# High and low fp32r parts for the recurrence gates' products in a one-core decoder step

## The chip, the cores and the metric

The kernel runs on one core of a Trainium2 chip. The metric is the device time of one execution in microseconds (us), from several timed executions. One further execution was taken by the hardware profiler, and the rows below come from it.

## The reference

One step of a hybrid decoder: 512 prompt tokens and 32 sample tokens (8 sequences of 4), model width 1024. A mixer with two branches is followed by a mixture of experts. The change lies in the second branch, the RG-LRU recurrence, whose two gates are block-diagonal products: eight blocks of 128 channels, each with one 128x128 matrix per gate.

```python
def block_diag_linear(x, w, b):
    xb = x.reshape(x.shape[:-1] + (H_B, BLK_B))          # H_B = 8 blocks of BLK_B = 128
    y = jnp.einsum('bshi,hij->bshj', xb, w) + b
    return y.reshape(x.shape)

def rg_lru(x, h0, lam, w_a, b_a, w_x, b_x):
    r = jax.nn.sigmoid(block_diag_linear(x, w_a, b_a))
    i = jax.nn.sigmoid(block_diag_linear(x, w_x, b_x))
    log_a = -LRU_C * r * jax.nn.softplus(-lam)
    a = jnp.exp(log_a)
    mult = jnp.sqrt(-jnp.expm1(2.0 * log_a))
    bt = mult * (i * x)
    ...                                                   # h[t] = a[t] * h[t-1] + bt[t]

def mixer_sublayer(...):
    u, v, xr, g_a, g_b = jnp.split(rms_norm(x, norm_g) @ w_in, SPLITS, axis=-1)
    y_a = gelu(u) * spatial_gating(layer_norm(gelu(v)))
    xc, new_buf = causal_depthwise_conv(xr, conv_buf, conv_w, conv_b)    # 4 taps
    y_b, h_last = rg_lru(xc, h0, ...)
    merged = jax.nn.sigmoid(g_a) * y_a + jax.nn.sigmoid(g_b) * y_b
    return x + merged @ w_out, h_last, new_buf, v_rows
```

## The kernel before

The program is written engine by engine, each engine with its own instruction list in a fixed order; semaphores tie the lists together, and no scheduler moves anything. Its stages in time are: normalising and transposing the tokens, the v projection (8 weight units), a loop over 8 channel tiles of 128 channels, the output projection (16 units), routing, and the experts, whose weights stream in by DMA.

The projections are made in fp32r, a format in which TensorE needs one pass for a product. To keep fp32 accuracy a product is split: ScalarE writes the high part of a weight unit (`split_hi`, line 697: `wh` from `raw`), VectorE the low part (`split_lo`, line 906: `wl` = `raw` - `wh`), and `product` (lines 1475 to 1477) makes high times high, high times low and low times high into the same PSUM bank.

The loop over channel tiles (`channel_tile` on TensorE, `channel` on VectorE, a loop of the same length on ScalarE) has four projection units per tile, p = 0 to 3, each 24 fp32r products of 128x512:

- First the 32 sample rows of all four units (line 1594), which need the four raw weight tiles that the sync engine's queue loads ahead (line 474).
- Unit 0 gives the recurrence's input. ScalarE copies it to `XR` (semaphore `xr_ev`), and VectorE makes the four-tap convolution `XC` from it (lines 1056 to 1070) and then raises `conv_done`.
- Unit 1 gives u, and unit 2 the first branch's output gate.
- After unit 2 TensorE waits for `conv_done` and makes the two recurrence gates (lines 1626 and 1627): for each gate w a plain fp32 product of `gw[:, w]` with the 512 prompt columns of `XC`, and one with the 32 sample columns. `gw`, two 128x128 matrices, is loaded for each tile by GpSimd's queue (line 624) once the tile before has used it. In the first tile the spatial mixing of the v branch (lines 1578, 1583) stands between unit 1 and unit 2.
- Unit 3 gives the second output gate.
- ScalarE turns the gates into a and the square root that the recurrence needs; for that it waits for `gates_mm` and, later, for the end of unit 3. VectorE then makes the scan and the merge (lines 1085 to 1112), splits weights in between, and goes round the loop.

On VectorE, `own.then(instruction)` issues an instruction and waits until it has finished. Tiles 0 to 6 are a hardware loop; the last one is written out after it, with the output projection's first `split_lo` calls in between.

Of the kernel before, what the change touches and what calls it, by code (L numbers as in the profile page):

```python
# [22 lines left out]
P = 128  # L23
D = 1024
KT = D // P
SEQ = 512
# [39 lines left out]
F32 = mybir.dt.float32  # L66
F32R = mybir.dt.float32r
# [3 lines left out]
ALU = mybir.AluOpType  # L71
# [37 lines left out]
def build(nc, x, wmix, wgate, chan, wst, bs, rows, wr, br, wmoe, y, vp, vs, st):  # L109
# [3 lines left out]
    def at(name, offset, shape, dt=F32):  # L113
        return nc.alloc_sbuf_tensor_at(name, shape, dt, offset=BASE + offset)

    K = 1024
# [58 lines left out]
    top = [181 * K]  # L175

    def small(name, shape, dt=F32):
        size = 4
        for n in shape[1:]:
            size *= n  # L180
        t = at(name, top[0], shape, dt)
        top[0] += -(-size // 32) * 32
        return t
# [6 lines left out]
    late = top[0]  # L190
# [3 lines left out]
    gw = small("gw", [P, 2, P])  # L194
# [30 lines left out]
    rstd = small("rstd", [P, TILES])  # L225
    ssa = small("ssa", [P, TILES])
    lg = small("lg", [P, TILES, NL])
    r4 = small("r4", [P, TILES, NG])
    oh = small("oh", [P, TILES, NG])
    r1 = small("r1", [P, 8, TILES])  # L230
    key = small("key", [P, TILES, NE])
    ohe = small("ohe", [P, 2, TILES, NE])
    mcnt = small("mcnt", [P, TILES, NE], BF16)
    cum = small("cum", [P, TILES + 1, NE], BF16)
    onesb = small("onesb", [P, P], BF16)
# [29 lines left out]
    with ExitStack() as ctx:  # L265
        ps = ctx.enter_context(nc.psum_tensor("ps", [P, 8, 512], F32))

        def sem(name):
            return ctx.enter_context(nc.semaphore(name))
# [8 lines left out]
        gw_in = sem("gw_in")  # L278
# [619 lines left out]
        def _(d):  # L898
            own = Steps(d, dve_s)
# [150 lines left out]
            def channel(j, last):  # L1050
# [2 lines left out]
                n0 = UNITS_V  # L1053

                d.wait_ge(gates_mm, FIRST + j)
                own.then(d.tensor_copy(xrs[:, :, 0:3], col(C_ST, 24).rearrange("p (b s) -> p b s", b=DB)))
                d.wait_ge(xr_ev, FIRST + j * 2 + 2)
                own.then(d.tensor_scalar(XC[:, 0:SEQ], XR[:, 3:3 + SEQ], col(C_W0 + 3), col(C_CB), ALU.mult, ALU.add))
                own.then(d.tensor_scalar(smp(XC), xrs[:, :, 3:7], col(C_W0 + 3), col(C_CB), ALU.mult, ALU.add))
                for t in range(3):  # L1060
# [4 lines left out]
                    if t < 2:  # L1065
                        own.then(i)
                own.then(i)
                sj = so[:, bass.ds(j, 1), :].rearrange("p a c -> p (a c)")
                d.tensor_copy(sj[:, 9:12], XR[:, SEQ:SEQ + 3])
                d.tensor_copy(sj[:, 12:36].rearrange("p (b s) -> p b s", b=DB), xrs[:, :, 4:7]).then_inc(conv_done, 1)  # L1070
# [47 lines left out]
                    split_lo(0, 2, j * 4 + (n0 + 7))  # L1118

            with d.Fori(0, KT - 1) as j:  # L1120
                own.enter(j, 25)
                channel(j, False)
                own.leave(KT - 1)
            channel(KT - 1, True)

            def add_rows(half, p, bank):
# [338 lines left out]
        def _(pe):  # L1465
# [7 lines left out]
            def product(out, sh, sl, mh_, ml_, start, stop):  # L1473

                pe.matmul(out, sh, mh_, start=start, stop=False)  # L1475
                pe.matmul(out, sl, mh_, start=False, stop=False)  # L1476
                return pe.matmul(out, sh, ml_, start=False, stop=stop)  # L1477
# [36 lines left out]
            def nothing(*_):  # L1514
                pass
# [53 lines left out]
            def z_mixing():  # L1569

                pe.wait_ge(masks, 7)
                pe.wait_ge(v_gelu, 2 * TILES)
                pe.wait_ge(v_ready, 1 + TILES)
                for c8 in range(KT):
                    if c8 >= 4:
                        pe.wait_ge(z_ready, c8 - 3)
                    for c in range(NT):
                        i = pe.matmul(ps[:, ZB[c8 % 4], c * P:(c + 1) * P], v[:, c, c8 * P:(c8 + 1) * P], wsT[:, c8 // 2, :],  # L1578
                                      start=True, stop=True)
                    i.then_inc(z_mm, 1)  # L1580
                pe.wait_ge(z_ready, 5)
                for c8 in range(KT):
                    i = pe.matmul(ps[:, ZB[0], c8 * S:(c8 + 1) * S], v[0:S, NT, c8 * P:(c8 + 1) * P], bdiag[:, c8 // 2, :],
                                  start=True, stop=True)
                i.then_inc(z_mm, 1)
                pe.wait_ge(z_ready, KT)

            def channel_tile(j, z_here):
                for s in range(RAW):
                    pe.wait_ge(raw_in[s], j * 16 + 48)  # L1590
                pe.wait_ge(sproj_sb, FIRST + j)
                for k in range(KT):
                    q = k % 4
                    i = pe.matmul(ps[S * q:S * q + S, 6, :].rearrange("p (u c) -> p u c", u=4), xs[:, k, :], raw[:, :, k, :],  # L1594
                                  start=k < 4, stop=k >= 4, tile_position=(0, S * q), skip_group_check=True)
                i.then_inc(sproj, 1)
                for p, freed in enumerate((xr_ev, u_ev, ga_ev, None)):
                    pe.wait_ge(hi_ready, j * 4 + (UNITS_V + p + 1))
                    pe.wait_ge(lo_ready, j * 4 + (UNITS_V + p + 1))
                    if z_here and p < 2:  # L1600
                        pe.wait_ge(v_gelu, 2 * TILES - 2 + p)
                    if freed is not None:
                        pe.wait_ge(freed, FIRST + j * 2)
                    else:
                        pe.wait_ge(merged, FIRST + j)
                    for k in range(KT):
                        c = slice(k * P, k * P + P)
                        i = product(ps[:, p, :], wh[:, p % 2, c], wl[:, p % 2, c], xh[:, k, :], xl[:, k, :], k == 0, k == KT - 1)
                    i.then_inc(unit_done, 1)
                    if p == 1 and z_here:  # L1610
                        z_mixing()
                    if p == 0:

                        pe.wait_ge(sproj_sb, FIRST + j + 1)
                        pe.wait_ge(gates_ev, FIRST + j * 4)
                        for u in range(4):
                            i = pe.matmul(ps[:, 7, u * S:(u + 1) * S], sp[:, u * P:(u + 1) * P], fold[:], start=True, stop=True)
                        i.then_inc(sproj_T, 1)
                    if p == 2:
                        pe.wait_ge(conv_done, FIRST + j + 1)  # L1620
                        pe.wait_ge(gw_in, j * 16 + 16)
                        pe.wait_ge(sq_sb, j + 1)
                        pe.wait_ge(z_ready, 2 * KT)
                        pe.wait_ge(gates_ev, FIRST + j * 4)
                        for w in range(2):
                            pe.matmul(ps[:, 4 + w, :], gw[:, w, :], XC[:, 0:SEQ], start=True, stop=True)  # L1626
                            i = pe.matmul(ps[:, 7, (4 + w) * S:(5 + w) * S], gw[:, w, :], XC[:, SEQ:TA], start=True, stop=True)
                        i.then_inc(gates_mm, 1)

            channel_tile(0, True)  # L1630
            with pe.Fori(1, KT) as j:
                channel_tile(j, False)
# [140 lines left out]
            for s in range(2):  # L1773
                for p in range(TILES):
                    r = rowsof(TILE_AT[p])
                    for part in range(3):
                        l = pe.matmul(ps[:, 4, 0:PAIRS], posh[0:r, s, p, :], rsk[0:r, part, s, p, :],
                                      start=s + p + part == 0, stop=s == 1 and p == TILES - 1 and part == 2)
# [180 lines left out]
```

## Time and profile before

| what | value |
|---|---|
| median of 3 runs | 658.03 us (654.76, 658.03, 659.07) |
| the profiled execution's own time | 657.93 us |
| span of the profiled execution | 656.3 us |
| TensorE busy | 602.3 us, 92% of the span |
| VectorE busy | 322.6 us, 49% |
| ScalarE busy | 229.1 us, 35% |
| one channel tile (start of its gate products to the next one's) | 27.0 us, from 159.47 to 186.51 us |

The span covers the instructions of the core; the time of an execution is 1.6 us longer. Busy shares are averages over all stages; what counts for an edit in one stage is which wait ends last there.

### The profile page before, as it was taken

Reading aid. Unit: us, or ns where it says so; the run is one execution under the profiler, and the core shown is the slowest. Engines: PE = TensorE matmul, PEld = TensorE weight load, DVE = VectorE, ACT = ScalarE, POOL = GpSimd, SP = SyncE. Lnnn points to the kernel's source line nnn. Section 1 sums busy time; section 2 is a strip of 40 time slices with the busy share of each in tenths; the row PEclk is TensorE's granted clock in tenths of the full one; section 3 lists DMA queues with packets and bytes.
Section 4 is the critical chain, followed back from the end, with each engine's and each line's share of the span. In section 5 each row is a group of like instructions: output and inputs, shape, how many; then the busy total and the mean of one; then the engine's idle time right before and its main releaser. Section 6 shows DMA issues by size and latency. Waiting matters only on the chain.

```text
span 656.3 us, 8891 instructions
## 1 busy us (share of the span) xinstructions
PE 602.3 (92%) x2860; PEld 360.1 (55%) x2860; DVE 322.6 (49%) x672; ACT 229.1 (35%) x393; POOL 51.6 (8%) x126
## 2 busy tenths in 40 slices
PE   6899999999999999999999888999999878987893
PEld 3676696877778777787578633433333323332320
DVE  4834687767777677686555763110010002110157
ACT  5423425465573755738353311111111111110114
POOL 1100010000000000000000021121212111111000
PEclk9899999999999999999997978999999999999977
DMA  8411324832122322232692589999999999999973
GB/s 313 159 70 65 128 81 167 354 105 70 65 72 96 104 72 81 60 108 79 219 417 85 196 329 423 418 419 420 419 420 422 419 419 420 421 417 421 401 295 136
DMA packets 33447, 160.60 MB, mean 245 GB/s; under 512 B 6320, under 2 KB 6704, under 8 KB 21008
## 3 DMA queue, kind: packets, MB, share of 16 engines
q1 hardware_dynamic: 27808, 149.52, 57.8%
q0 software_dynamic: 5472, 10.63, 4.4%
q8 instruction: 14, 0.23, 0.2%
q10 hardware_dynamic: 144, 0.15, 0.1%
q14 instruction: 9, 0.07, 0.0%
HBM read 155.01 MB, written 14.17 MB: 258 GB/s over the span
## 4 chain that ended last, share of the span: by engine, by line
PE 61%; SPq 18%; DVE 9%; DMA 6%; ACT 3%; issue 3%; DVEq 0%; ACTq 0%
SPq L536 15%; PE ps L1475 13%; PE ps L1477 12%; PE ps L1476 12%; PE ps L1818 6%; DMA wslot<-in_wmoe 4%; PE ps L1844 4%; PE ps L1594 2%; PE ps L1626 2%; PE ps L1680 1%; DMA raw<-in_wmix 1%; SPq L569 1%; DVE wl L906 1%; PE ps L1578 1%; PE ps L1881 1%
## 5 line engine op out<-in xcount | busy, mean ns | idle before, releaser
L1818 PE MATMUL ps<-wslot,xgT 128*64 128x512 f32 x528 | 123.8, 601 | 13.4 <-DMA wslot<-in_wmoe 12.0
L697 ACT ACTIVATE wh<-raw 128x1024 fp32r<-128x1024 f32 x56 | 59.1, 1057 | 155.9 <-PE ps L1477 139.2
L1475 PE MATMUL ps<-xh,wh 128*128 128x512 f32 x256 | 102.4, 400 | 0.0
L1477 PE MATMUL ps<-xl,wh 128*128 128x512 f32 x256 | 99.9, 390 | 0.0
L1476 PE MATMUL ps<-xh,wl 128*128 128x512 f32 x256 | 99.9, 390 | 0.0
L906 DVE TENSOR_TENSOR wl<-raw,wh 128x1024 fp32r<-128x1024 f32 x56 | 68.5, 1223 | 47.2 <-ACT wh L697 46.2
L1818 PEld LDWEIGHTS ps<-wslot,xgT 128*64 128x64 f32 x528 | 40.8, 138 | 91.4 <-issue 89.6
L1844 PE MATMUL ps<-wslot,hT 128*64 128x512 f32 x264 | 63.8, 612 | 8.6 <-ACT hT L867 7.7
L1391 DVE SCALAR_TENSOR_TENSOR hm<-ps,rt,hs 128x256 f32<-128x256 f32 x12 | 5.8, 484 | 126.6 <-ACT hs L865 126.6
L1475 PEld LDWEIGHTS ps<-xh,wh 128*128 128x128 f32 x256 | 48.1, 188 | 16.1 <-issue 6.7
L1477 PEld LDWEIGHTS ps<-xl,wh 128*128 128x128 f32 x256 | 48.1, 188 | 10.6
L1476 PEld LDWEIGHTS ps<-xh,wl 128*128 128x128 f32 x256 | 48.1, 188 | 9.4
L1844 PEld LDWEIGHTS ps<-wslot,hT 128*64 128x64 f32 x264 | 18.9, 139 | 42.6 <-issue 30.0
L870 ACT ACTIVATE yo<-ps 128x1024 f32<-128x1024 f32 x17 | 17.4, 1024 | 67.4 <-PE ps L1844 67.4
L865 ACT ACTIVATE hs<-ps,rt 128x256 f32<-128x256 f32 x12 | 5.7, 476 | 85.4 <-PE ps L1818 85.4
L1391 DVE SCALAR_TENSOR_TENSOR hm<-ps,rtx,hs 128x256 f32<-128x256 f32 x5 | 2.4, 484 | 57.9 <-ACT hs L865 57.9
L1475 PE MATMUL ps<-wh,xh 128*128 128x512 f32 x64 | 27.1, 423 | 3.1 <-DVE xs L932 2.1
L1475 PE MATMUL ps<-wh,mh 128*128 128x512 f32 x64 | 27.3, 426 | 0.1
L1477 PE MATMUL ps<-wl,mh 128*128 128x512 f32 x64 | 26.0, 406 | 0.0
L1476 PE MATMUL ps<-wh,ml 128*128 128x512 f32 x64 | 25.9, 405 | 0.0
L1477 PE MATMUL ps<-wl,xh 128*128 128x512 f32 x64 | 25.9, 405 | 0.0
L1476 PE MATMUL ps<-wh,xl 128*128 128x512 f32 x64 | 25.9, 405 | 0.0
(330 smaller groups left out, 795.1 us busy)
## 6 DMA issues: line engine op xcount, KB each, us to landing
wslot<-in_wmoe SPq DMA_DIRECT2D x97, 1024.0 KB, 26.5
raw<-in_wmix SPq DMA_DIRECT2D x56, 512.0 KB, 4.0
gy<-ytok SPq DMA_DIRECT2D x8, 512.0 KB, 7.3
xt<-in_x SPq DMA_DIRECT2D x4, 512.0 KB, 6.9
x<-in_x SPq DMA_DIRECT2D x4, 512.0 KB, 5.0
xnd<-x SPq DMA_DIRECT2D x4, 512.0 KB, 5.8
wslot<-in_wmoe SPq DMA_DIRECT2D x4, 512.0 KB, 26.9
out_y<-yf SPq DMA_DIRECT2D x4, 512.0 KB, 2.6
```

What stands on the lines that cost most here:

```text
L536: e.dma_start(wslot[q][s][:, lo:hi], wmoe[bass.ds(number + s, 1), :, lo:hi].rearrange("a p c -> (a p) c")).then_inc(part_in[part][q][s], 16)
L697: a.activation(WH[hslot], raw[:, slot, :, :].rearrange("p k c -> p (k c)"), ACT.Copy).then_inc(hi_ready, 1)
L870: a.activation(yo[:], ps[:, 6:8, :].rearrange("p b c -> p (b c)"), ACT.Copy).then_inc(yo_sb, 1)
L906: d.tensor_tensor(WL[hslot], raw[:, slot, :, :].rearrange("p k c -> p (k c)"), WH[hslot].bitcast(F32), ALU.subtract).then_inc(lo_ready, 1)
L1391: d.scalar_tensor_tensor(out=hm[:], in0=ps[:, 2, FE:2 * FE], scalar=scale, in1=hs[:], op0=ALU.mult, op1=ALU.mult).then_inc(hm_ready, 1)
L1475: pe.matmul(out, sh, mh_, start=start, stop=False)
L1476: pe.matmul(out, sl, mh_, start=False, stop=False)
L1477: return pe.matmul(out, sh, ml_, start=False, stop=stop)
L1594: i = pe.matmul(ps[S * q:S * q + S, 6, :].rearrange("p (u c) -> p u c", u=4), xs[:, k, :], raw[:, :, k, :], start=k < 4, stop=k >= 4, tile ...
L1626: pe.matmul(ps[:, 4 + w, :], gw[:, w, :], XC[:, 0:SEQ], start=True, stop=True)
L1818: l = pe.matmul(ps[CAP * s:CAP * s + CAP, 2, :], xgT[:, c, CAP * s:CAP * s + CAP], wslot[q][s][:, c * 512:(c + 1) * 512], start=c == 0, st ...
L1844: l = pe.matmul(ps[CAP * s:CAP * s + CAP, 6 + h, :], hT[:, f, CAP * s:CAP * s + CAP], wslot[q][s][:, o:o + 512], start=f == 0, stop=f == 1 ...
```

## The change

The two 128x512 gate products are no longer made in plain fp32. VectorE makes high and low fp32r parts of the tile's two gate matrices (`gwh`, `gwl`, 128x256 each) at the head of `channel`, and of the convolution's prompt columns (`xch`, `xcl`, 128x512 each) right behind the convolution, ahead of `conv_done`. TensorE calls `product` on them, three fp32r products for each gate. The products with the 32 sample columns stay as they were. VectorE also waits for the gate matrices' load (`gw_in`) now, which only TensorE did. The new tiles lie in space that other tiles use later or used earlier, and no other tile moves.

```diff
+    gwh = at("gwh", router, [P, 2, P], F32R)
+    gwl = at("gwl", router + K, [P, 2, P], F32R)
+    xch = at("xch", late, [P, SEQ], F32R)
+    xcl = at("xcl", late + 2 * K, [P, SEQ], F32R)
...
                 d.wait_ge(gates_mm, FIRST + j)
+                d.wait_ge(gw_in, j * 16 + 16)
+                own.then(d.tensor_copy(gwh[:], gw[:]))
+                own.then(d.tensor_tensor(gwl[:], gw[:], gwh[:].bitcast(F32), ALU.subtract))
                 own.then(d.tensor_copy(xrs[:, :, 0:3], col(C_ST, 24).rearrange("p (b s) -> p b s", b=DB)))
                 d.wait_ge(xr_ev, FIRST + j * 2 + 2)
...
                 own.then(i)
+                own.then(d.tensor_copy(xch[:], XC[:, 0:SEQ]))
+                own.then(d.tensor_tensor(xcl[:], XC[:, 0:SEQ], xch[:].bitcast(F32), ALU.subtract))
                 sj = so[:, bass.ds(j, 1), :].rearrange("p a c -> p (a c)")
...
-                own.enter(j, 25)
+                own.enter(j, 29)
...
                         for w in range(2):
-                            pe.matmul(ps[:, 4 + w, :], gw[:, w, :], XC[:, 0:SEQ], start=True, stop=True)
+                            product(ps[:, 4 + w, :], gwh[:, w, :], gwl[:, w, :], xch[:], xcl[:], True, True)
                             i = pe.matmul(ps[:, 7, (4 + w) * S:(5 + w) * S], gw[:, w, :], XC[:, SEQ:TA], start=True, stop=True)
```

VectorE before, from the end of the convolution to the split of unit 3's weights, in every tile (rows without a tile name, as L88 and ISA, are register arithmetic and waits):

```order
L1061 SCALAR_TENSOR_TENSOR xc<-xr,ch,xc 128x512
L88 REGISTER_ALU
L1063 SCALAR_TENSOR_TENSOR xc<-xr,ch,xc 128x32
L88 REGISTER_ALU
L1069 ISA
L1069 COPY so<-xr 128x3
L1070 ISA
L1070 COPY so<-xr 128x24
L905 ISA
L906 TENSOR_TENSOR wl<-raw,wh 128x1024
```

The same place after the change (`conv_done` is raised by the last COPY):

```order
L1070 SCALAR_TENSOR_TENSOR xc<-xr,ch,xc 128x512
L88 REGISTER_ALU
L1072 SCALAR_TENSOR_TENSOR xc<-xr,ch,xc 128x32
L88 REGISTER_ALU
L1077 CAST xch<-xc 128x512
L88 REGISTER_ALU
L1078 TENSOR_TENSOR xcl<-xc,xch 128x512
L88 REGISTER_ALU
L1080 ISA
L1080 COPY so<-xr 128x3
L1081 ISA
L1081 COPY so<-xr 128x24
```

Two instructions of 128x512 now stand between the convolution and `conv_done`, each followed by a wait for its own end. The head of `channel` after the change, ahead of the convolution:

```order
L1062 ISA
L1063 CAST gwh<-gw 128x256
L88 ISA
L1064 TENSOR_TENSOR gwl<-gw,gwh 128x256
L88 REGISTER_ALU
L1065 ISA
L1065 COPY xr<-ch 128x8x3
```

Before, the loop's first instruction was the COPY; two instructions of 128x256 with a wait behind each now stand ahead of it. TensorE before, between unit 2 and unit 3:

```order
L1477 MATMUL ps<-xl,wh 128x512
L1626 MATMUL ps<-xc,gw 128x512
L1627 MATMUL ps<-xc,gw 128x32
L1626 MATMUL ps<-xc,gw 128x512
L1627 MATMUL ps<-xc,gw 128x32
L1475 MATMUL ps<-xh,wh 128x512
```

and after the change:

```order
L1488 MATMUL ps<-xl,wh 128x512
L1486 MATMUL ps<-xch,gwh 128x512
L1487 MATMUL ps<-xch,gwl 128x512
L1488 MATMUL ps<-xcl,gwh 128x512
L1638 MATMUL ps<-xc,gw 128x32
L1486 MATMUL ps<-xch,gwh 128x512
L1487 MATMUL ps<-xch,gwl 128x512
L1488 MATMUL ps<-xcl,gwh 128x512
L1638 MATMUL ps<-xc,gw 128x32
L1486 MATMUL ps<-xh,wh 128x512
```

Each fp32 product of 128x512 has become three fp32r ones; nothing else moved on TensorE.

## Rows read from the trace of the kernel before

**Rows 1.** The page: TensorE's busy time, and the chain that ended last.

```profile
PE 602.3 (92%) x2860; PEld 360.1 (55%) x2860; DVE 322.6 (49%) x672; ACT 229.1 (35%) x393; POOL 51.6 (8%) x126
PE 61%; SPq 18%; DVE 9%; DMA 6%; ACT 3%; issue 3%; DVEq 0%; ACTq 0%
```

**Rows 2.** TensorE's timeline, one tile's gates: start, duration (us), line, operation [idle before].

```profile
186.51 1.02 PE L1626 MATMUL ps<-xc,gw 128*128 128x512 f32 x2
187.37 0.30 PE L1627 MATMUL ps<-xc,gw 128*128 128x32 f32 x2
187.50 1.10 PE L1626 MATMUL ps<-xc,gw 128*128 128x512 f32 x2
188.59 0.48 PE L1475 MATMUL ps<-xh,wh 128*128 128x512 f32 x1
188.90 0.40 PE L1476 MATMUL ps<-xh,wl 128*128 128x512 f32 x1
189.13 0.40 PE L1477 MATMUL ps<-xl,wh 128*128 128x512 f32 x1
...
194.25 1.92 PE L1594 MATMUL ps<-raw,xs 128*32 128x512 f32 x16
```

**Rows 3.** VectorE's timeline of the same tile, from the merge to beyond the gates.

```profile
176.40 0.43 DVE L1110 CAST mh<-m 128x512 f32 x1
176.97 0.18 DVE L1111 COPY ms<-m 128x32 f32 x1
177.28 0.69 DVE L1112 TENSOR_TENSOR ml<-m,mh 128x512 f32 x1
...
184.26 0.18 DVE L1070 COPY so<-xr 128x24 f32 x1
...
187.87 1.23 DVE L906 TENSOR_TENSOR wl<-raw,wh 128x1024 fp32r<-128x1024 f32 x1 [1.16 <-ACT wh L697]
190.45 0.72 DVE L1078 SCALAR_TENSOR_TENSOR u<-u,u 128x544 f32<-128x544 f32 x1 [1.35 <-ACT u L780]
```

**Rows 4.** VectorE's timeline, first tile: the instruction that raises `conv_done`.

```profile
105.13 0.18 DVE L1070 COPY so<-xr 128x24 f32 x1
```

**Rows 5.** TensorE's timeline, first tile: the first gate product.

```profile
105.36 1.12 PE L1626 MATMUL ps<-xc,gw 128*128 128x512 f32 x2 [1.58 <-DVE so L1070]
```

**Rows 6.** TensorE's timeline, first microseconds: two longer idle times.

```profile
12.38 1.06 PE L1529 MATMUL ps<-ident,xt 128*128 128x128 f32 x8 [2.58 <-DVE wl L906]
...
24.26 0.77 PE L1475 MATMUL ps<-wh,xh 128*128 128x512 f32 x1 [2.08 <-DVE xs L932]
```

**Rows 7.** Windows: busy us (instructions) by engine, granted clock, DMA share, GB/s.

```profile
13.00:14.00 1.00, 0.91 (x6) 0.68 (x4) 0.67 (x3) 0.37 (x2) 0.00 (x0) 0.73 1.04 418
...
16.00:17.00 1.00, 1.00 (x7) 0.80 (x6) 0.67 (x3) 0.20 (x1) 0.00 (x0) 0.56 1.04 414
...
25.00:26.00 1.00, 1.00 (x4) 0.81 (x3) 0.88 (x4) 0.00 (x0) 0.20 (x3) 0.50 0.06 16
```

**Rows 8.** Windows, with the same columns, behind the first tile's first gate products.

```profile
107.00:110.00 3.00, 3.00 (x15) 2.34 (x14) 2.86 (x4) 2.25 (x6) 0.55 (x1) 1.00 0.82 257
```

**Rows 9.** TensorE's timeline at the lower granted clock, output projection.

```profile
346.75 0.63 PE L1477 MATMUL ps<-wl,mh 128*128 128x512 f32 x1
347.18 0.63 PE L1475 MATMUL ps<-wh,mh 128*128 128x512 f32 x1
```

**Rows 10.** Last tile: VectorE's timeline, the instruction that raises `conv_done`.

```profile
291.59 0.17 DVE L1070 COPY so<-xr 128x24 f32<-128x24 f32 x1
```

**Rows 11.** Last tile: TensorE's timeline, the first gate product.

```profile
294.64 1.02 PE L1626 MATMUL ps<-xc,gw 128*128 128x512 f32 x2
```

**Rows 12.** Line 474, the raw weight loads between 140 and 290 us.

```profile
DMA to landing us min/median/max: 3.2/3.4/4.6
```

**Rows 13.** Tile `gw`: its eight loads, from issue to landing.

```profile
DMA to landing us min/median/max: 2.3/2.3/6.0
```

**Rows 14.** GpSimd's timeline: the first `gw` load.

```profile
92.54 0.59 POOL L624 DMA_DIRECT2D gw<-in_wgate  x1 [0.42 <-issue]
```

More of the change, by code:

```diff
@@ L227, in build @@
     lg = small("lg", [P, TILES, NL])
+    router = top[0]
     r4 = small("r4", [P, TILES, NG])
@@ L232, in build @@
     ohe = small("ohe", [P, 2, TILES, NE])
+    gwh = at("gwh", router, [P, 2, P], F32R)
+    gwl = at("gwl", router + K, [P, 2, P], F32R)
+    assert top[0] >= router + 2 * K
+    xch = at("xch", late, [P, SEQ], F32R)
+    xcl = at("xcl", late + 2 * K, [P, SEQ], F32R)
     mcnt = small("mcnt", [P, TILES, NE], BF16)
```

## The prediction

> **What bounds the kernel now.** I read the page's busy times first: TensorE is busy for 602.3 us of 656.3, and the chain that ended last runs on it for 61% of the span [rows 1]. Then I read TensorE's timeline in the loop over channel tiles, since the change touches nothing else. There the reader is to see that one product follows the other without idle time, also at the gates: the first gate product carries no idle time at 186.51 us [rows 2], while it does in the first tile, 1.58 us behind VectorE's line 1070 [rows 5]. So in the loop TensorE sets the time, and in the first tile, for that one moment, VectorE does. Last I read VectorE's timeline of the same tile [rows 3], for the question on which all depends: how early is `conv_done`? Line 1070 ends at 184.26 + 0.18 = 184.44 us, and TensorE starts the gates at 186.51. The margin is 2.07 us. VectorE has no idle time between the recurrence's end and that point, so whatever is put ahead of line 1070 comes out of this margin. Its idle time lies behind: 1.16 us ahead of a weight split and 1.35 us ahead of line 1078 [rows 3].
>
> **What TensorE gains.** A fp32 product and its 128x32 companion take 187.50 - 186.51 = 0.99 us the first time and 188.59 - 187.50 = 1.09 the second, 2.08 together. The companion alone is 187.50 - 187.37 = 0.13, so a fp32 product is 0.86 and 0.96 [rows 2]. In fp32r, starts are 0.31 us apart behind a plain fp32 product (188.59 to 188.90) and 0.23 otherwise (188.90 to 189.13) [rows 2]. The new block is 3 x 0.23 + 0.13 for the first gate and 0.31 + 2 x 0.23 + 0.13 for the second: 0.82 + 0.90 = 1.72 us. The gain is 2.08 - 1.72 = 0.36 us a tile, 2.9 us over eight tiles if nothing else moved.
>
> The row shows a fp32 product at 0.86 us, 3.7 spacings of 0.23. The Trainium skill, FP8 and Floating Point Precision, section TensorE Precision Notes, says that true fp32 takes four passes through the array; four passes of 0.23 would be 0.92 and the gain a tile 0.06 to 0.1 us off mine. The row is used.
>
> **What VectorE pays.** Four instructions a tile are added ahead of `conv_done`, each waited for. The pair on `XC` has its twin in the merge: the 128x512 cast takes 0.43 us and the subtraction 0.69 [rows 3]. The pair on `gw` is 128x256, which no row shows between SBUF tiles. It lies between the 128x32 copy, 0.18, and the 128x512 cast, 0.43: by the straight line 0.30. The subtraction lies between 0.18, what the smallest of these rows takes, and 0.69 for 512: 0.43. The wait behind each leaves 176.97 - 176.40 - 0.43 = 0.14 us [rows 3]. In all 0.43 + 0.69 + 0.30 + 0.43 + 4 x 0.14 = 2.41 us. Bounds: with the `gw` pair at the 128x32 row (0.18 each) and gaps of 0.10 it is 1.9; with the pair as dear as the 128x512 one (1.12) and the gaps at 0.2 it is 3.0. I take 2.41, as 256 columns lie midway between those ends.
>
> For the cast the row has 0.43 us at 512 columns. The Trainium skill, VectorE: DVE Perf Modes, section on the TRN2 errata, gives a copy between SBUF tiles as 58 cycles plus half the columns at 0.96 GHz, which by estimate is 0.33 us for 512 columns and 0.19 for 256; with these the added work would be 2.2 us and the end 1.3 us earlier. The trace disagrees at 512 columns (0.43), and the measurement decides.
>
> **Tiles 1 to 6.** VectorE's chain starts anew in each tile from ScalarE's square root, which waits for the end of unit 3, so it is measured from TensorE's own progress. 2.41 us more against a margin of 2.07 leaves TensorE waiting for 0.34; the lag from line 1070's end to the gate's start adds 105.36 - 105.31 = 0.05 [rows 4, 5]; and a gate that was waited for starts with its weights not yet loaded: 1.12 us against 1.02 [rows 2, 5], 0.10 more. So each tile pays 0.49 and gains 0.36: +0.13 us, and +0.8 over six. VectorE's delay doesn't carry into the next tile: its later idle times, 1.16 + 1.35 = 2.51 us, take up 2.41. The margin that covers this is thin, 0.1 us; beyond it ScalarE's square root would still wait for unit 3.
>
> **The first tile.** VectorE is already late, so nothing hides the 2.41 us. The weights weren't preloaded before either, so it costs 2.41 - 0.36 = +2.05 us.
>
> **The clock.** The first tile's idle time grows from 1.58 to about 4.0 us. After idle times of 2.58 and 2.08 us early in the kernel [rows 6] the granted clock was 0.73 and then 0.50, the 1.2 GHz level [rows 7]; after 1.58 us in the first tile it stayed at 1.00, the 2.4 GHz level [rows 8]. So 4.0 us will likely lower it. At the lower level fp32r products start 347.18 - 346.75 = 0.43 us apart instead of 0.23 [rows 9]. The first low stretch runs from about 13.5 to 16.9 us: with 1.00 and 0.50 as the only levels, 0.73 from 13 to 14 us puts the fall at 13.46, and 0.56 from 16 to 17 the rise at 16.88 [rows 7]. In 3.4 us some 8 products fit, which take 1.8 us at the higher level: 1.6 us lost at most, and nothing is lost for the part of the stretch that falls into the idle time. Bounds 0 and 1.6, taken 1.2.
>
> **The last tile** is outside the loop. `conv_done` comes at 291.76 and the gates start at 294.64 [rows 10, 11], a margin of 2.88 us that holds 2.41. It gains up to 0.36, but what follows is VectorE's merge behind ScalarE, which gains less: taken -0.2.
>
> **What costs nothing.** The added wait for `gw`: its loads land 2.3 us after issue, at most 6.0 [rows 13], and the first is issued at 92.54 [rows 14], so it is there by 98.5 at the latest, before the channel loop starts in VectorE's list near 99.5; later ones have over 10 us. Unit 3's weight split is queued behind `conv_done` and moves from 185.6 to 188.0 us; TensorE wants it when the gates end, at about 188.7. That split also frees the raw tile whose reload the next tile's first products need at 194.25 [rows 2]: 188.0 + 0.3 + 3.4, or at worst 4.6 [rows 12], is 193 at most.
>
> **Sum.** 657.93 (the profiled execution's own time, 0.1 below the median) + 2.05 + 1.2 + 0.8 - 0.2 = 661.8 us. Everything behind the loop waits for TensorE's last projection or is queued behind it, so the shift reaches the end whole.
>
> **Rivals.**
> 1. *The clock holds.* The lower level doesn't come, or its stretch falls into the idle time: 660.6. For it: 1.58 us of idle did nothing. Against: 2.08 us did.
> 2. *VectorE's parts are cheaper*, 1.9 to 2.0 us. Then tiles 1 to 6 have no wait and each keeps 0.36: first tile +1.6, six tiles -2.2, last -0.3, so 657.0, or 658.2 with the clock's term. It ends below the time before, by less than can be measured. For a gain of over 1%, 6.6 us, even all eight gains of 0.36 don't do; with eight fp32 blocks of 2.08 = 16.6 us in all, the new block would have to cost 1.2 us in place of 1.72 and the first tile nothing.
> 3. *VectorE becomes the loop's bound outright (slower).* Behind `conv_done` VectorE has 2.51 us of idle time for 2.41 of work. If the four instructions and gaps cost 3.0, 0.6 us a tile is waited for more at the gates and 0.5 is left over past line 1078, of which ScalarE may pass some on: first tile +2.6, six tiles 6 x (0.72 to 1.1) = 4.3 to 6.6, clock 1.2: 666 to 668. It decides at 2.5 us of added work; the merge's twins speak against.
> 4. *The parts aren't made as written*, with the products lowered as plain fp32: three at 0.86 in place of one would cost 16 x 1.7 = 27 us, 685. The instruction lists show the same `product` as the projections', whose rows have 0.23; I give this 1 in 100.
>
> **Chances.** The forecast 0.55; rival 1 0.2; rival 2 0.13; rival 3 0.11; rival 4 0.01. No change can be told from runs within about 1% here, 651.4 to 664.6. The range from 656.5 to 666.0 takes in rivals 1 and 2 and the cheaper part of rival 3. Slower by over 1% is rival 4, most of rival 3 and the forecast with a large clock term: 0.11. Faster by over 1% has no mechanism: 0.02.
>
> **What would show it.** In the changed trace: gate blocks of about 1.7 us; a wait of 0.3 to 0.5 us for VectorE's line that raises `conv_done`, in tiles 1 to 6 and not in the last; an idle time near 4.0 us in the first tile and a granted clock of 0.50 behind it; tile periods of 27.1 to 27.2 us. No wait in the loop and periods near 26.7 would say that VectorE's parts were priced too high; idle time ahead of unit 3, or ahead of the sample rows' products, that I missed a thing queued behind `conv_done`.

## The result, and the profile after

| | before | after |
|---|---|---|
| median of 20 runs | 657.02 us (654.04 to 659.29) | 660.85 us (657.78 to 666.68) |
| ratio | | 1.0066, 95% interval 1.0048 to 1.0084 |
| span of the profiled execution | 656.3 us | 657.8 us |

By the ratio the changed kernel is slower by 4.3 us (3.2 to 5.5 by the interval), 0.66%; the two medians are 3.8 us apart. The forecast was 3.9 us slower. The span of the one profiled execution has grown by 1.5 us only; the end of this section says why.

TensorE's timeline of the changed kernel, in the first, the second and the third tile: start, duration (us), line, operation [idle before and what ended it].

```profile
107.20 0.50 PE L1486 MATMUL ps<-xch,gwh 128*128 128x512 f32 x1 [3.64 <-DVE so L1081]
...
116.30 1.93 PE L1605 MATMUL ps<-raw,xs 128*32 128x512 f32 x16
...
135.97 0.47 PE L1486 MATMUL ps<-xch,gwh 128*128 128x512 f32 x1 [0.26 <-issue]
...
163.12 0.47 PE L1486 MATMUL ps<-xch,gwh 128*128 128x512 f32 x1 [0.23 <-issue]
163.43 0.40 PE L1487 MATMUL ps<-xch,gwl 128*128 128x512 f32 x1
163.66 0.40 PE L1488 MATMUL ps<-xcl,gwh 128*128 128x512 f32 x1
163.90 0.30 PE L1638 MATMUL ps<-xc,gw 128*128 128x32 f32 x2
164.03 0.48 PE L1486 MATMUL ps<-xch,gwh 128*128 128x512 f32 x1
...
164.95 0.48 PE L1486 MATMUL ps<-xh,wh 128*128 128x512 f32 x1
```

Three things are to be seen. The first tile's idle time is 3.64 us where it was 1.58 [rows 5]. Where the gates followed unit 2 without idle time [rows 2], there are now 0.2 to 0.3 us of it in every tile of the loop. And the block of the two gates itself takes 164.95 - 163.12 = 1.83 us, against 2.08 before.

VectorE's timeline of the second tile, the same columns; this answers to [rows 3].

```profile
128.10 0.29 DVE L1063 CAST gwh<-gw 128x256 fp32r<-128x256 f32 x1
128.42 0.43 DVE L1064 TENSOR_TENSOR gwl<-gw,gwh 128x256 fp32r<-128x256 f32 x1
129.01 0.18 DVE L1065 COPY xr<-ch 128x24 f32 x1 [0.16 <-DVE gwl L1064]
...
134.00 0.43 DVE L1077 CAST xch<-xc 128x512 fp32r<-128x512 f32 x1
134.46 0.69 DVE L1078 TENSOR_TENSOR xcl<-xc,xch 128x512 fp32r<-128x512 f32 x1
135.31 0.17 DVE L1080 COPY so<-xr 128x3 f32 x1 [0.16 <-DVE xcl L1078]
135.44 0.18 DVE L1081 COPY so<-xr 128x24 f32 x1
135.56 1.23 DVE L912 TENSOR_TENSOR wl<-raw,wh 128x1024 fp32r<-128x1024 f32 x1
...
137.82 1.22 DVE L912 TENSOR_TENSOR wl<-raw,wh 128x1024 fp32r<-128x1024 f32 x1
139.49 0.73 DVE L1089 SCALAR_TENSOR_TENSOR u<-u,u 128x544 f32<-128x544 f32 x1 [0.45 <-ACT u L786]
```

The four new instructions last 0.29, 0.43, 0.43 and 0.69 us. The idle time that stood behind `conv_done` before, 1.16 and 1.35 us [rows 3], is down to 0.45: it has taken up the added work, and nothing goes into the next tile.

The granted clock, from windows of the changed kernel (the columns are those of [rows 7]), behind the first tile's idle time and around the output projection's first router products:

```profile
108.00:110.00 2.00, 2.00 (x7) 1.66 (x6) 1.97 (x4) 0.53 (x1) 0.00 (x0) 0.50 0.22 33
110.00:112.00 2.00, 2.00 (x9) 1.68 (x8) 1.86 (x3) 1.48 (x5) 0.55 (x1) 0.74 0.99 381
...
343.00:348.00 5.00, 5.00 (x42) 4.39 (x40) 2.96 (x7) 1.87 (x4) 0.00 (x0) 1.00 1.02 397
348.00:353.00 5.00, 5.00 (x40) 4.08 (x40) 0.77 (x5) 1.06 (x1) 0.00 (x0) 1.00 0.72 290
```

The same two last windows in the kernel before:

```profile
343.00:348.00 5.00, 5.00 (x26) 4.55 (x26) 1.62 (x3) 0.07 (x1) 0.00 (x0) 0.66 0.97 384
348.00:353.00 5.00, 5.00 (x29) 3.61 (x28) 0.87 (x5) 1.06 (x1) 0.00 (x0) 0.66 0.03 13
```

Behind the first tile's idle time the clock was at its lower level (0.50, 1.2 GHz), as forecast. The second pair bears on why the two spans lie closer than the medians. Both kernels run 32 small fp32 products of 36 columns there, the kernel before first, the changed kernel second:

```profile
341.58 4.37 PE L1680 MATMUL ps<-wrt,xn2T 128*128 128x36 f32 x32
...
345.19 3.76 PE L1691 MATMUL ps<-wrt,xn2T 128*128 128x36 f32 x32
```

Before, the clock fell while they ran (0.78 from 344 to 345 us) and stayed at 0.50 until after 351; in the changed kernel it stayed at 1.00. TensorE's list in that place is the same in both, and the channel loop ended some 40 us earlier. The changed kernel was 3.6 us late at the start of these products and 0.5 late at the first fp32r product after the low stretch (352.36 against 351.88), so about 3.1 us of the loss are hidden in this one execution by a low stretch that only the kernel before had. Further on the difference changes again: the changed kernel is 0.6 us early at 411 us, when another low stretch has passed in the kernel before, 1.0 late at 565, behind products that waited for expert weights, and 1.5 late at the end. A difference of two spans alone would have given the change a third of its cost.

### The profile page after: what moved, and what is told of

Read it like the earlier page. It is cut to its first block, busy times and chain, and to the rows that moved or that the text cites. A ratio compares the mean times of both kernels' runs of the same rounds, so it can differ in the third digit from the quotient of the medians.

```text
span 657.8 us, 8991 instructions
## 1 busy us (share of the span) xinstructions
PE 596.2 (91%) x2876; PEld 360.2 (55%) x2876; DVE 336.6 (51%) x704; ACT 229.0 (35%) x393; POOL 51.7 (8%) x126
## 4 chain that ended last, share of the span: by engine, by line
PE 55%; SPq 16%; DVE 12%; DMA 9%; ACT 4%; issue 4%; DVEq 0%; ACTq 0%; POOLq 0%
SPq L542 14%; PE ps L1486 13%; PE ps L1488 12%; PE ps L1487 12%; PE ps L1829 6%; DMA wslot<-in_wmoe 5%; PE ps L1855 4%; PE ps L1605 2%; DMA gy<-ytok 2%; DVE wl L912 1%; DMA ytok<-yo,idx 1%; DMA raw<-in_wmix 1%; PE ps L1691 1%; PE ps L1589 1%; PE ps L1628 1%
## 5 line engine op out<-in xcount | busy, mean ns | idle before, releaser
L1855 PE MATMUL ps<-wslot,hT 128*64 128x512 f32 x264 | 62.1, 598 | 8.7 <-ACT hT L873 7.7
```

Of the source, the lines that this page charges most:

```text
L1855: l = pe.matmul(ps[CAP * s:CAP * s + CAP, 6 + h, :], hT[:, f, CAP * s:CAP * s + CAP], wslot[q][s][:, o:o + 512], start=f == 0, stop=f == 1 ...
```

## The experiments

The starts of the sample products at the head of a tile (line 1605 after the change, line 1594 before) measure a tile's period. The table has them for all kernels, worked out from their timelines: from tile 0 to tile 1, and the mean of the six periods after that.

| kernel | tile 0 to 1, us | later periods, us | timed ratio to before, 95% interval |
|---|---|---|---|
| before | 38.69 | 27.03 | |
| after | 42.02 | 27.15 | 1.0066 (1.0048 to 1.0084) |
| parts made, plain products | 42.43 | 27.48 | 1.0115 (1.0087 to 1.0143) |
| fp32r products, no parts | 38.38 | 26.65 | |
| extra products in first tile | 40.46 | 27.15 | 1.0060 (1.0038 to 1.0082) |
| `conv_done` waited for last | 42.11 | 26.95 | 1.0078 (1.0048 to 1.0109) |
| gate matrices' parts only, plain products | 41.23 | 27.03 | |
| their parts in idle time, wait last | 41.60 | 26.71 | 1.0005 (0.9984 to 1.0026) |
| the same, extra products in first tile | 40.07 | 26.71 | 0.9991 (0.9969 to 1.0013) |
| the same parts, first tile plain | 37.60 | 26.71 | 0.9949 (0.9928 to 0.9971) |
| before, first tile written out | 37.59 | 27.03 | 0.9991 (0.9969 to 1.0013) |

The two kernels without a ratio were timed in one execution each.

**The parts alone.** The parts are made as in the changed kernel and not used.

```diff
-                            product(ps[:, 4 + w, :], gwh[:, w, :], gwl[:, w, :], xch[:], xcl[:], True, True)
+                            pe.matmul(ps[:, 4 + w, :], gw[:, w, :], XC[:, 0:SEQ], start=True, stop=True)
```

> The changed kernel with VectorE's four new instructions left in every tile, but the gate products back in plain fp32 (the parts are made and not used). My theory, that VectorE's work ahead of conv_done costs the time and the fp32r products give 0.36 us a tile back: first tile idle for about 3.6 us with a granted clock of 0.50 behind it, tile period 27.15 + 0.36 = 27.5 us, time before + 2.1 + 1.5 + 6 x 0.48 = before + 6.5 us. Rival, that the fp32r products cost and not the parts (more weight loads, a switch of format): tile period 27.03 and the time of before.

Measured: period 27.48, first tile 3.74 us longer than before, ratio 1.0115: 7.5 us slower (5.7 to 9.4). TensorE's timeline in the third tile and in the first:

```profile
108.63 1.96 PE L1637 MATMUL ps<-xc,gw 128*128 128x512 f32 x2 [3.64 <-DVE so L1081]
...
165.33 1.10 PE L1637 MATMUL ps<-xc,gw 128*128 128x512 f32 x2 [0.23 <-issue]
```

The idle times are those of the changed kernel to 0.01 us, with other products behind them. With plain products behind them the cost is still there, so VectorE's work is the cost, and the rival is out. By the periods it costs 3.7 + 6 x 0.45 = 6.4 us.

**The products alone.** The three products take slices of `xh` and `xl`, and VectorE makes no parts. The edit is shown against the kernel before.

```diff
-                            pe.matmul(ps[:, 4 + w, :], gw[:, w, :], XC[:, 0:SEQ], start=True, stop=True)
+                            product(ps[:, 4 + w, :], xh[:, w, 0:P], xl[:, w, 0:P], xh[:, 2 + w, :], xl[:, 2 + w, :], True, True)
```

> The changed kernel with the three fp32r products for each gate, but without VectorE's four instructions: the products take slices of xh and xl, so the gates' values are not those of the reference and the routing may differ; only the channel tiles are to be read. My theory: no wait in tiles 1 to 6, tile period 27.03 - 0.36 = 26.67 us, first tile idle 1.6 us and no fall of the clock there. Rival, that the products give nothing in place: 27.03 us.

```profile
166.18 1.92 PE L1600 MATMUL ps<-raw,xs 128*32 128x512 f32 x16
...
192.83 1.92 PE L1600 MATMUL ps<-raw,xs 128*32 128x512 f32 x16
```

The period is 26.65, 0.38 us below 27.03: the products give what they were forecast to give, 0.36. In the first tile the idle time is 1.58 us as before. (The time of the whole kernel says nothing here, since the routing is another.)

**The clock in the first tile.** Four fp32 products are put ahead of TensorE's wait.

```diff
+                    if p == 2 and z_here:
+                        pe.wait_ge(z_ready, 2 * KT)
+                        keep_warm(4, 4, ones)
                     if p == 2:
                         pe.wait_ge(conv_done, FIRST + j + 1)
```

> The changed kernel with four fp32 products of 128x512 on a free bank (3.5 us) ahead of TensorE's wait in the first tile, and nothing else. My theory, that the idle time of 3.64 us in the first tile lowers the clock and costs 1.3 to 1.5 us: granted clock 1.00 from 107 to 111 us, first tile's gates not later than 107.2 us, tile 1's sample products 1.3 to 1.5 us earlier than in the changed kernel (116.3 us), time before + 2.5. Rival, that the clock falls there for another reason (the fp32r products behind plain ones): it falls all the same and the time is before + 4.

TensorE's timeline:

```profile
104.90 3.60 PE L1482 MATMUL ps<-ones 128*128 128x512 f32 x8
108.71 0.50 PE L1486 MATMUL ps<-xch,gwh 128*128 128x512 f32 x1 [0.21 <-DVE so L1081]
...
116.23 1.92 PE L1605 MATMUL ps<-raw,xs 128*32 128x512 f32 x16
```

and its clock, from windows:

```profile
108.00:110.00 2.00, 1.79 (x9) 1.11 (x8) 1.84 (x5) 0.27 (x2) 0.00 (x0) 1.00 0.00 0
```

The clock holds, and from the gates' start to the next tile's head it is 116.23 - 108.71 = 7.52 us, against 116.30 - 107.20 = 9.10 in the changed kernel. The lower level costs 1.58 us, and it is the idle time that brings it: the rival had the fp32r products to blame, which are all there, and with plain products behind the same idle time the clock fell too (parts alone, 0.50 from 109 to 112 us). The timed ratio, 1.0060, is lower than the changed kernel's 1.0066, but the intervals overlap; 1.6 us is little against them, and the trace carries this finding.

**The order of TensorE's waits.** In the changed kernel the instruction that raises `conv_done` ends at 135.44 + 0.18 = 135.62 and the gates start at 135.97, 0.35 us later, while in the first tile the lag is 107.20 - 107.15 = 0.05.

```diff
-                        pe.wait_ge(conv_done, FIRST + j + 1)
                         pe.wait_ge(gw_in, j * 16 + 16)
                         pe.wait_ge(sq_sb, j + 1)
                         pe.wait_ge(z_ready, 2 * KT)
                         pe.wait_ge(gates_ev, FIRST + j * 4)
+                        pe.wait_ge(conv_done, FIRST + j + 1)
```

> The changed kernel with TensorE's five waits ahead of the gates in another order: the wait for conv_done last instead of first, so that the four others, which are long fulfilled, are done while TensorE still works. In the changed kernel the gates of tiles 1 to 6 start 0.35 us after the instruction that raises conv_done has ended, in the first tile 0.05 us. Theory A, that the rest, 0.3 us, is TensorE's sequencer working through the four waits behind: tile period 27.15 - 0.3 = 26.85 us, time before + 2.5. Theory B, that 0.35 us is what a release inside the loop takes: tile period 27.15, time before + 4.

The third tile, VectorE's and TensorE's timelines:

```profile
162.62 0.18 DVE L1081 COPY so<-xr 128x24 f32 x1
...
162.94 0.47 PE L1486 MATMUL ps<-xch,gwh 128*128 128x512 f32 x1
```

The lag falls from 0.35 to 162.94 - 162.80 = 0.14 us and the period from 27.15 to 26.95. Theory A holds with 0.2 us in place of 0.3: in the loop, waits that are long fulfilled still take time if they stand behind the one that is not. In the first tile, which is written out on TensorE, it is the other way round: with the wait for `conv_done` first the lag is 0.05 us, with it last 0.15 (107.45 behind a copy that ends at 107.12 + 0.18 = 107.30). So the new order helps in the loop and costs 0.1 us outside it. Six times 0.2 are 1.2 us; the timed ratio, 1.0078, doesn't show them and its interval is wide enough (4 us) to hide them.

**Half the parts, plain products.** The two instructions for XC are left out, and the products are plain.

```diff
-                own.then(d.tensor_copy(xch[:], XC[:, 0:SEQ]))
-                own.then(d.tensor_tensor(xcl[:], XC[:, 0:SEQ], xch[:].bitcast(F32), ALU.subtract))
...
+                            pe.matmul(ps[:, 4 + w, :], gw[:, w, :], XC[:, 0:SEQ], start=True, stop=True)
```

> The changed kernel with the two instructions for the gate matrices' parts left at the head of each tile, without the two for XC, and with the gate products in plain fp32 (the parts are made and not used). 0.9 us stand ahead of conv_done. By the margin of 2.07 us they are hidden in tiles 1 to 6: period 27.03 us, as before; the first tile's idle time grows from 1.58 to 2.5 us, with or without a fall of the clock. If every added microsecond on VectorE cost its length, the period would be 27.9.

```profile
106.15 1.12 PE L1635 MATMUL ps<-xc,gw 128*128 128x512 f32 x2 [2.45 <-DVE so L1079]
...
108.00:110.00 2.00, 2.00 (x6) 1.22 (x5) 2.00 (x3) 1.04 (x2) 0.00 (x0) 0.50 0.80 264
```

The period is 27.03, as before: 0.9 us of added work ahead of `conv_done` cost nothing in the loop. The margin is real. In the first tile the idle time is 2.45 us, and that is enough for the lower clock (a timeline row, and a row of the windows).

**The parts of the gate matrices in idle time.** They are made for the next tile ahead of line 1100, where VectorE waits for ScalarE's square root, and for the first tile between the two groups of z instructions (not shown); the wait for `conv_done` is last (not shown, as above).

```diff
-                d.wait_ge(gw_in, j * 16 + 16)
-                own.then(d.tensor_copy(gwh[:], gw[:]))
-                own.then(d.tensor_tensor(gwl[:], gw[:], gwh[:].bitcast(F32), ALU.subtract))
...
                 split_lo(1, 1, j * 4 + (n0 + 6))
+                if not last:
+                    d.wait_ge(gates_mm, FIRST + j + 1)
+                    d.wait_ge(gw_in, j * 16 + 32)
+                    own.then(d.tensor_copy(gwh[:], gw[:]))
+                    own.then(d.tensor_tensor(gwl[:], gw[:], gwh[:].bitcast(F32), ALU.subtract))
                 d.wait_ge(m_sqrt, j + 1)
...
```

With the four extra products in the first tile:

> The changed kernel with three edits: the parts of the gate matrices are made for the next tile in VectorE's idle time ahead of line 1100 (for the first tile between the two groups of z instructions), so that only the 1.2 us for the parts of XC stands ahead of conv_done; the wait for conv_done last on TensorE; and four fp32 products on a free bank ahead of the first tile's wait. My theory: 1.2 us fits into the margin of 2.07, so tiles 1 to 6 have a period of 27.03 - 0.38 = 26.65 us as with the products alone; first tile +1.2 - 0.4 = +0.8, last -0.3; before - 1.8 us, ratio 0.997, which would beat both kernels. Rival, that work put ahead of line 1100 comes back there, since the square root's user starts later: period 27.0 or more and a time at or above before.

and without them:

> The same without the four extra products in the first tile. TensorE's idle time there should be 1.58 + 1.2 = 2.8 us. If an idle time of that length lowers the clock, as 2.58 us did early in the kernel, the first tile costs 1 to 1.6 us more than with the extra products (time at that of before); if the clock holds, nothing (before - 1.8).

VectorE's timeline of the second one:

```profile
103.10 0.75 DVE L1070 SCALAR_TENSOR_TENSOR xc<-xr,ch,xc 128x512 f32<-128x512 f32 x1 [0.51 <-DVE xc L1072]
...
118.50 0.28 DVE L1102 CAST gwh<-gw 128x256 fp32r<-128x256 f32 x1
118.82 0.42 DVE L1103 TENSOR_TENSOR gwl<-gw,gwh 128x256 fp32r<-128x256 f32 x1
120.06 0.06 DVE L1105 MEMSET m<- 128x1 f32 x1 [0.81 <-ACT m L806]
```

Idle time of 0.81 us is still left where the parts now are, and both kernels have the period 26.71: six times 0.32 us below the kernel before. The rival, that the work comes back there, is out. The first tile takes most of it back: 40.07 - 38.69 = 1.4 us with the extra products, where 0.8 were expected. Without them its idle time is 3.30 us where 2.8 were expected, the clock falls, and it is 41.60. The rest is the same in both: between two taps of the convolution in the first tile VectorE was idle for 0.51 us (the first row above), where it is about 0.15 in the other kernels with this loop, and the wait for `conv_done` in last place costs 0.1. Both kernels with the early parts have the 0.51 and none of the others does, so it belongs to this edit; why is open. The ratios, 0.9991 and 1.0005, are both "no change"; the first misses the expected 0.997, which lies at the edge of its interval, and with -0.3 us for the last tile, as in the changed kernel, the trace gives 1.4 - 1.9 - 0.3 = -0.8 us, ratio 0.999.

**The first tile left plain.** The last step follows from these: as in the two kernels before, but parts of XC and fp32r products only from the second tile on, and no gate matrices' parts for the first. The third argument of `channel` leaves out the parts of XC.

```diff
-            with d.Fori(0, KT - 1) as j:
+            channel(0, False, True)
+            own.base -= 29
+            with d.Fori(1, KT - 1) as j:
...
-                            product(ps[:, 4 + w, :], gwh[:, w, :], gwl[:, w, :], xch[:], xcl[:], True, True)
+                            if z_here:
+                                pe.matmul(ps[:, 4 + w, :], gw[:, w, :], XC[:, 0:SEQ], start=True, stop=True)
+                            else:
+                                product(ps[:, 4 + w, :], gwh[:, w, :], gwl[:, w, :], xch[:], xcl[:], True, True)
```

> The gate matrices' parts in VectorE's idle time and the wait for conv_done last, as in the two kernels before, but the first tile keeps its plain fp32 gate products and makes no parts of XC; for that VectorE's first tile is written out ahead of the loop, where its waits cost about 0.1 us each less. My theory: the first tile's idle time is at most that of before (1.58 us) and the clock holds there, tiles 1 to 6 have a period of 26.7 us, the last gains 0.3: 6 x 0.32 + 0.3 = 2.2 us, and up to 0.9 for the written out first tile: before - 2.2 to - 3.1, ratio 0.995 to 0.997. Rival, that a gain in the loop is lost behind it, as the other version's ratio of 0.999 leaves open: ratio 1.000.

and its control, the kernel before with nothing but VectorE's first tile written out:

> Control for the other: the kernel before with VectorE's first tile written out ahead of its loop and nothing else. If the written out tile is what helps, the first tile's idle time falls from 1.58 to about 0.7 us and the ratio is 0.999; the tile periods stay at 27.03. If it does nothing, 1.000.

TensorE's timeline, the first kernel's and the control's first gates:

```profile
104.50 1.10 PE L1643 MATMUL ps<-xc,gw 128*128 128x512 f32 x2 [0.55 <-DVE so L1079]
```

```profile
104.07 1.13 PE L1628 MATMUL ps<-xc,gw 128*128 128x512 f32 x2 [0.46 <-DVE so L1070]
```

The first is at 0.9949 (0.9928 to 0.9971), 3.4 us faster than the kernel before; the changed kernel's interval lies above 1, so it beats that one too. The control is at 0.9991, not to be told from no change, though its first tile is 1.1 us shorter in the trace (idle time 0.46 in place of 1.58). Against its control the new kernel's median is 2.3 us lower (653.08 and 655.42, 12 executions each), and the two first tiles are alike (37.60 and 37.59). So the written out tile accounts for 1.1 of the 3.4 us by the trace; the timed control leaves room for none or for up to 2.0. The rest goes with the fp32r products, of which the trace has 6 x 0.32 = 1.9 us in the loop.

## Why the prediction was right

The forecast was 661.8 us, 3.9 above the time before; measured were 4.3 (3.2 to 5.5). The mechanism was right: VectorE's parts use up the margin in the loop, and nothing hides them in the first tile. That the number is so close is in part luck, since errors cancel in two places. By its own steps:

- *What TensorE gains*, 0.36 us a tile: 0.38 by the products alone (26.65 against 27.03). Right. In the changed kernel the block takes 1.83 us, 0.11 above the forecast's 1.72; the forecast had put down 0.10 for weights that aren't loaded yet when a gate was waited for. One side sum of the forecast doesn't come out: two products of 0.92 are 1.84 us against the rows' 0.86 + 0.96 = 1.82, which moves the gain by 0.02 and not by 0.06 to 0.1.
- *What VectorE pays*, 2.41 us: too high. From the weight split ahead of the convolution to the copy that raises `conv_done`, start to start, it is 135.44 - 126.96 = 8.48 us now and was 130.21 - 123.85 = 6.36: 2.12 us. The durations were right to 0.01 us (0.43, 0.69, 0.29 for 0.30, 0.43 for 0.43). The gaps were not: behind the four instructions they are 0.03, 0.16, 0.03 and 0.16 us, and the gap behind the convolution, 0.16 before, is 0.04 now, so together they add about 0.28 where 4 x 0.14 = 0.56 was taken from one gap of the merge. The copy row of the cycle table in the Trainium skill, VectorE: DVE Perf Modes, section on the TRN2 errata, which the prediction used for its second sum, gives by estimate 0.19 us for 256 columns; the trace has 0.29. The same section says under its table that the measured fixed term is about 150 cycles in place of 58; with that the estimate is 0.29 and 0.42 us for 256 and 512 columns, and the trace (0.29 and 0.43) agrees. The prediction passed this over. Its second sum is off besides: 0.21 us less work in the first tile and in six more is 1.5 us, not 1.3.
- *Tiles 1 to 6*, +0.13 us each: +0.12 measured, but by two errors that cancel. The parts are 0.29 us cheaper, and the lag from VectorE's end to the gates' start is 0.35 us and not the 0.05 of the first tile, of which 0.2 go when the four waits behind the one that ends last are put ahead of it; in the kernel before, `conv_done` came 2.07 us early and all five could be done while TensorE worked. The sum of the measured terms is 0.05 (2.12 against 2.07) + 0.35 + 0.10 - 0.38 = +0.12. With that wait last the lag is 0.14, the same sum gives -0.09, and the period is 26.95, 0.08 below the kernel before. This step was right in its number and incomplete in its mechanism.
- *The first tile*, +2.05 us, and *the clock*, +1.2 (bounds 0 and 1.6): together 3.33 measured (42.02 - 38.69). The clock's share is 1.58 by the extra products, at its upper bound: the granted clock is 0.80 from 107 to 108 us and 0.50 after it, which puts the fall at 107.6, behind the end of the idle time at 107.20, so none of the low stretch lay in the idle time. The rest is 1.75: an idle time 3.64 - 1.58 = 2.06 us longer, less the gates' gain. So the clock was put 0.4 too low and the rest 0.3 too high, and the two cancel.
- *The last tile*, -0.2 us: from the last tile's head to the output projection's sample products it is 319.48 - 279.18 = 40.30 us, against 315.94 - 275.35 = 40.59 before: -0.29.
- *Sum*: 3.33 + 6 x 0.12 - 0.29 = 3.8 us by the trace, which the timed 4.3 holds. *That the shift reaches the end whole* agrees with the medians but isn't shown: the two traces can't show it, as the clock and the waits for expert weights differ behind the loop.
- *What costs nothing*: no wait for `gw_in` or for raw tiles appears, and the half-parts experiment shows the margin hiding 0.9 us.

Rival 1 (the clock holds) is out: it fell after idle times of 2.45, 3.30, 3.64 and 3.74 us in the first tile. Rival 2 (cheaper parts, 1.9 to 2.0 us) came near, with 2.12, but even with the wait for `conv_done` last the period, 26.95, stays above its 27.03 - 0.36 = 26.67. Rivals 3 and 4 are out: the loop has 0.45 us of VectorE's idle time left, and the products have the projections' durations.

What stays open: whether the chance of a low clock at the router's small products differs between the kernels, and how much of the 4.3 us it makes. Of the eleven traces, six have the fall there (before, its first tile written out, extra products, `conv_done` waited for last, gate matrices' parts only, first tile plain) and five have not (after, parts alone, products alone, both with early parts). Where it came, the stretch from these products to the next sample rows' was 1.6 to 3.2 us longer, up to three quarters of what the change costs.

## What to carry to other kernels

A cheaper product on the busiest engine is worth its gain only if the engine that prepares its operands has that much slack ahead of the handover; here 0.38 us a tile were bought with 2.1 us against a margin of 2.07, and in the first tile against none. Split the preparation by what it depends on: the parts of the weights could go into idle time elsewhere, only those of the fresh activations had to stand ahead of the handover, and a first tile that is already late is left as it was. In a hardware loop, put the wait that ends last at the end of a row of waits; in code that is written out it stood better first. And compare stages of two traces, not their spans: one stretch of low clock behind the changed stage hid 3.1 of 3.6 us.

## What the runs showed of the hardware

- TensorE's granted clock was at 0.50 behind idle times of 2.45, 3.30, 3.64 and 3.74 us in the same place, and at 1.00 behind 0.46 to 1.58 us. One fall cost 1.58 us of the products behind it.
- It also fell without any idle time just before, during 32 fp32 products of 36 columns, in five of eleven traces (in a sixth an idle time of 1.27 us stood shortly ahead of them), and held in the same place in five.
- Of a row of five waits in a hardware loop, four of them fulfilled, those behind the unfulfilled one delayed the engine by 0.2 us (lag 0.35 against 0.14). In the tile outside the loop the unfulfilled wait in first place gave a lag of 0.05 us, in last place 0.15. Why it differs was not tested.
- Where VectorE waited for an instruction's own end in the loop, the gap behind it was 0.03 to 0.04 us or 0.12 to 0.17, and where the convolution also waits for ScalarE's copy 0.31. In the tile that is written out they are 0.03 to 0.05. In the lists above, a short gap stands ahead of lines 1072, 1077 and 1078, which have no ISA row of their own, a long one (0.16) ahead of lines 1065 and 1080, which have one. So the long gap goes with what the next instruction needs in the loop, and not with the kind of the instruction before it; this is a reading of lists and gaps, and no run tests it.
